# Startup loads, order of the modulation groups, start points of small jobs and of the context stream in a fused two-block transformer kernel

## The reference, cut to what matters

```python
for l in range(2):                                    # first block
    x = layer_norm(a * x + 0.5 * swiglu_ffn(x, w_in[l, 0], w_out[l, 0]), ...)
    x = layer_norm(a * x + mixer_sublayer(x, ...), ...)
    x = layer_norm(a * x + memory_cross_attention(x, mem, ...), ...)
    x = layer_norm(a * x + 0.5 * swiglu_ffn(x, w_in[l, 1], w_out[l, 1]), ...)
for l in range(2):                                    # second block; the context's last use is as keys of layer 1
    sh_a, sc_a, g_a, sh_f, sc_f, g_f = split(silu(cond) @ mod_w[l] + mod_b[l], 6)
    hx, hc = modulate(rms_norm(x), sh_a, sc_a), modulate(rms_norm(ctx), ...)
    y_x, y_c = even_mixer(hx, hc) if l == 0 else odd_mixer(hx, hc)
    x = x + g_a * (y_x @ w_out[l]);  x = x + g_f * swiglu(modulate(rms_norm(x), sh_f, sc_f), ...)
    # the context likewise, in layer 0 only
```

## Time and profile before

| | |
|---|---|
| median of 3 runs | 2775.28 us (2775.11 to 2776.57) |
| the profiled execution, its own time | 2772.24 us |
| its span, first to last instruction | 2770.4 us |
| mean granted TensorE clock | 0.986 |
| busy: PE, DVE, ACT, POOL | 2653.8, 1682.5, 1239.3, 171.5 us |

### The profile page before, as it was taken

How to read it: one execution, slowest core, us unless ns; L and a number is a source line. 1 busy time by engine, 2 the same in 40 slices (tenths; PEclk the granted TensorE clock), 3 DMA queues, 4 the chain that set the end, 5 groups by cost and what they waited for, 6 DMA issues and landing times. The chain is left out here.

```text
span 2770.4 us, 47510 instructions
## 1 busy us (share of the span) xinstructions
PE 2653.8 (96%) x16073; PEld 2215.4 (80%) x16073; DVE 1682.5 (61%) x2451; ACT 1239.3 (45%) x1731; POOL 171.5 (6%) x205
## 2 busy tenths in 40 slices
PE   8999999999989999999989998999999997899999
PEld 8987878879969978778688886877896884665898
DVE  5555675755545565767565767875664654755655
ACT  4444544444324445354344654555443442543443
POOL 0000000000120000000000201200000001100000
PEclk9999999999989999999999999999999998999999
DMA  7656455566766574456556535543555557433664
GB/s 235 187 186 188 130 163 182 191 213 190 203 212 199 163 233 127 142 171 202 200 182 184 154 122 169 164 141 106 162 187 185 198 163 209 138 99 122 206 190 137
DMA packets 250509, 480.32 MB, mean 173 GB/s; under 512 B 16697, under 2 KB 36225, under 8 KB 250273
## 3 DMA queue, kind: packets, MB, share of 16 engines
q1 hardware_dynamic: 239968, 444.19, 51.2%
q0 software_dynamic: 10304, 33.09, 4.2%
HBM read 470.37 MB, written 7.74 MB: 173 GB/s over the span
## 5 line engine op out<-in xcount | busy, mean ns | idle before, releaser
L121 DVE TENSOR_TENSOR wlo<-raw,whi 128x1024 fp32r<-128x1024 f32 (+2 forms) x786 | 914.2, 1173 | 766.5 <-ACT whi L162 618.7
L162 ACT ACTIVATE whi<-raw 128x1024 fp32r<-128x1024 f32 (+2 forms) x786 | 791.0, 1016 | 695.1 <-PE bank L170 533.5
L170 PE MATMUL bank<-xh,whi 128*128 128x256 f32 x2208 | 631.4, 286 | 16.5 <-DVE xl L121 9.4
L170 PE MATMUL bank<-xh,wlo 128*128 128x256 f32 x2208 | 627.2, 284 | 0.0
L170 PE MATMUL bank<-xl,whi 128*128 128x256 f32 x2208 | 626.3, 284 | 0.0
L170 PEld LDWEIGHTS bank<-xh,whi 128*128 128x128 f32 x2208 | 420.4, 190 | 33.9 <-issue 16.2
L170 PEld LDWEIGHTS bank<-xl,whi 128*128 128x128 f32 x2208 | 418.8, 190 | 1.1 <-issue 0.5
L170 PEld LDWEIGHTS bank<-xh,wlo 128*128 128x128 f32 x2208 | 419.2, 190 | 0.0
L170 PE MATMUL bank<-whi,xh 128*128 128x512 f32 (+2 forms) x632 | 257.5, 407 | 25.6 <-DVE wlo L121 6.7
L170 PE MATMUL bank<-wlo,xh 128*128 128x512 f32 (+2 forms) x632 | 248.8, 394 | 0.0
L170 PE MATMUL bank<-whi,xl 128*128 128x512 f32 (+2 forms) x632 | 248.7, 394 | 0.0
(11 more groups left out here) (415 smaller groups left out, 3841.9 us busy)
## 6 DMA issues: line engine op xcount, KB each, us to landing
raw<-in_ffn_w_in SPq DMA_DIRECT2D x280, 512.0 KB, 4.4
raw<-in_ffn_w_out SPq DMA_DIRECT2D x154, 512.0 KB, 4.3
raw<-in_w_mix_in SPq DMA_DIRECT2D x112, 512.0 KB, 3.6
raw<-in_mod_w SPq DMA_DIRECT2D x96, 512.0 KB, 4.7
raw<-in_od_w_in SPq DMA_DIRECT2D x40, 512.0 KB, 4.4
raw<-in_ffn_w_in SPq DMA_DIRECT2D x56, 256.0 KB, 2.8
raw<-in_w_branch SPq DMA_DIRECT2D x24, 512.0 KB, 3.6
raw<-in_ev_w_in SPq DMA_DIRECT2D x24, 512.0 KB, 3.7
```

The source lines that it names most:

```text
L121: return Made(self.e and self.e.tensor_tensor(out, a, b, op))
L162: return Made(self.e and self.e.activation(out, a, f, **k))
L170: return Made(self.e and self.e.matmul(out, lhs, rhs, **k))
```

## The change

x is loaded by SP in four pieces of 256 columns, ahead of and between the first weight blocks, and each piece is transposed on its own; the identity is loaded apart from the other constants, and the first layer norm's rows wait for these. The modulation groups go in another order, in which a gate's group never follows a gate's group, and the numbers that streams wait for follow. `rpb_scratch`, `tokens_of`, `dsa` and `choose_last` get one or more `yield`s. The context stream starts 12 us later by the planner. The context's values of the odd layer (two products, eight blocks) wait until x's feed-forward of the even layer is done. The odd layer's gate rows are loaded by a job.

```diff
+GROUPS = (0, 1, 2, 3, 4, 6, 5, 7, 8, 10, 9, 11)
+def for_norm(l, f):
+    return 12 * l + (11 if f else 4)
+def for_gate(l, f):
+    return 12 * l + (12 if f else 7)
@@ modulation
-        for j in range(12):
-            blk, half, i = j // 2, j % 2, j % 2
+        for place_, j in enumerate(GROUPS):
+            blk, half, i = j // 2, j % 2, place_ % 2
...
@@ setup
-    co.cdep = load_small(co, co.cst[:, :], A["consts"][:, :])
-    co.xready = load_small(co, co.x[:, :, :], A["x"][0].rearrange("(t p) d -> p t d", p=P))
-    load_ln(co, 0, 0)
-    co.xt.dep = to_t(co, lambda t, k: co.x[:, t, k * P:(k + 1) * P], 8, (co.xt.hi, co.xt.lo),
-                   (co.xready, co.cdep))
+    idep = load_small(co, co.cst[:, C_ID:C_ID + P], A["consts"][:, C_ID:C_ID + P])
+    co.cdep = load_small(co, co.cst[:, P:C_END], A["consts"][:, P:C_END])
...
+    for i in range(4):
+        cs = slice(256 * i, 256 * i + 256)
+        co.xready.append(co.sp.dma_start(co.x[:, :, cs], x[:, :, cs]).then_inc(co.s_x[i], by=16))
+        if i < AHEAD:
+            stage(co, i)
+        co.xt.dep += to_t(co, lambda t, k: co.x[:, t, (2 * i + k) * P:(2 * i + k + 1) * P], 2, ...)
+    load_ln(co, 0, 0, co.cdep)
@@ rpb_scratch
     a = co.dv.memset(z[:, :], 0.0).then_inc(co.s_dv)
+    yield
...
     for r in range(7):
+        yield
+        yield
         src = A["na_rpb_2"][0, :, r + 4, :]
@@ prenorm
-    yield from modulated(co, 12 * l + 6 * f + 4)
+    yield from modulated(co, for_norm(l, f))
@@ context
     ev.start(fe)
+    yield -12
...
     for c in range(2):
         yield from co.od.heads_gemm(1, 1, c, c1)
+    yield from until(co, "x fed")
+    for c in range(2):
         yield from co.od.values_gemm(1, c, c1)
@@ rows
     yield from ffn2(co, 0, 0, x2, gate, tiles)
+    co.passed.add("x fed")
...
+    gate = Gate(co.lg, co.pn.tile[:, 0:512], counts(co))
+    def gate_early():
+        while co.modulated < for_gate(1, 0):
+            yield
+        gate.make = gated(co, 1, 0, 0, gate)
+    early = spawn(co, gate_early())
     first = spawn(co, od.attend(0, co.Y, pr, at_, co.smo, co.mxo, counts(co), ya))
...
     last = spawn(co, od.attend(1, co.Y, pr, at_, co.smo, co.mxo, counts(co), yb))
-    yield from modulated(co, 18)
-    gate = Gate(co.lg, co.pn.tile[:, 0:512], counts(co))
-    make = gated(co, 1, 0, 0, gate)
-    yield from out_proj(co, 1, 0, 4, co.xt, make)
+    yield from modulated(co, for_gate(1, 0))
+    while not early.over:
+        yield 0
+    yield from out_proj(co, 1, 0, 4, co.xt, gate.make)
```

More of the change, by code:

```diff
@@ L224, in new_core @@
     co.s_out = sem("s_out")
+    co.s_x = [sem(f"s_x{i}") for i in range(4)]
     co.s_raw = [sem(f"s_raw{i}") for i in range(NRAW)]
@@ L241, in new_core @@
     co.bi = 0
-    for u in range(AHEAD):
-        stage(co, u)
     return co
@@ L803, in modulation @@
                 if late is not None and n == 1:
-                    m, half0, a, r = late
-                    rfree[r] = mod_columns(co, m // 12, m % 12 // 2, half0, rt[r], a)
-                    co.modulated, late = m + 1, None
+                    at, blk0, half0, a, r = late
+                    rfree[r] = mod_columns(co, at // 12, blk0, half0, rt[r], a)
+                    co.modulated, late = at + 1, None
                 yield took
@@ L814, in modulation @@
                     gate_bias(co, gates)
-                co.modulated = 12 * l + j + 1
+                co.modulated = 12 * l + place_ + 1
             else:
-                late = (12 * l + j, half, got[0], i)
+                late = (12 * l + place_, blk, half, got[0], i)
 def mod_columns(co, l, blk, half, rows, ready):
@@ L954, in setup @@
     co.xfree = co.rsfree = None
-    co.cdep = load_small(co, co.cst[:, :], A["consts"][:, :])
-    co.xready = load_small(co, co.x[:, :, :], A["x"][0].rearrange("(t p) d -> p t d", p=P))
-    load_ln(co, 0, 0)
-    co.xt.dep = to_t(co, lambda t, k: co.x[:, t, k * P:(k + 1) * P], 8, (co.xt.hi, co.xt.lo),
-                   (co.xready, co.cdep))
+    idep = load_small(co, co.cst[:, C_ID:C_ID + P], A["consts"][:, C_ID:C_ID + P])
+    co.cdep = load_small(co, co.cst[:, P:C_END], A["consts"][:, P:C_END])
+    x = A["x"][0].rearrange("(t p) d -> p t d", p=P)
+    co.xready, co.xt.dep = [], []
+    for i in range(4):
[3 more added lines that the diff above has]
+            stage(co, i)
+        co.xt.dep += to_t(co, lambda t, k: co.x[:, t, (2 * i + k) * P:(2 * i + k + 1) * P], 2,
+                          (co.xt.hi[:, 2 * i:2 * i + 2, :], co.xt.lo[:, 2 * i:2 * i + 2, :]), (co.xready[i], idep))
+    load_ln(co, 0, 0, co.cdep)
 def side_setup(co, fe):
@@ L973, in gen @@
         outs, made = [], []
-        co.dv.wait_ge(d, fe)
+        co.dv.wait_ge(d, fe, co.cdep)
         for h in range(8):
@@ L1793, in gated @@
 def gated(co, l, s, f, gate):
-    assert co.modulated >= 12 * l + 6 * f + 6
+    assert co.modulated >= for_gate(l, f)
     st = co.stream[s]
@@ L2384, in context @@
     yield from turned(co, room, 0, 8, tuple(done), c2, da_gain(co))
-    yield from modulated(co, 6)
+    yield from modulated(co, for_gate(0, 0))
     gate = Gate(at(74, "cgb", [P, D]), at(78, "cgw", [P, 512]), w["first block"])
@@ L2506, in rows @@
     yield from turned(co, co.Y, 4, 8, tuple(yb), co.xt)
-    yield from out_proj(co, 1, 4, 8, co.xt, make)
+    yield from out_proj(co, 1, 4, 8, co.xt, gate.make)
     co.limit, co.pn.free = 24, gate.free
```

## The result

| | median us | runs |
|---|---|---|
| before, beside it on the same chip | 2775.20 (2771.04 to 2776.78) | 6 |
| after | 2759.05 (2757.30 to 2761.66) | 6 |

The ratio is 0.9944, 95% interval 0.9931 to 0.9957: faster by 16 us, where 37 were forecast, and outside the range of 2720 to 2757. The profiled execution took 2757.32 us by its own time, with a span of 2755.5.

What follows compares the result with a forecast made beforehand. PE's own work was taken to bound the kernel, leaving its idle and half-clock time to win. Gains summed to 41.1 us, less 4.0 for new stalls: 2775.3 - 37.1 = 2738.2 us, range 2720 to 2757.

Steps and rivals of the forecast that it cites:

- Start: Kernel start: x loaded in pieces lets the first product start between 10.6 and 13.1 us; gain 0.5 us, from -0.5 to 4.0.
- One more block before a small job goes on: Mixer, both layers: an added product block covers PE's waits at `tk`, `ikt` and `choose_last`; gains 3.6, 1.8 and 8 us.
- DVE bounds the mixer: Rival: the mixer's stalls only move by a block; 13.4 us fewer gained, 2752 us; chance 0.12.
- about 1.6 us for each layer: Mixer, `choose_last`: stall left at the second score products, from stalls of 3.32 and 3.79 us, with PE arriving at about 363.2.
- The other terms, 3.6 and 1.8: Mixer, both layers: 3.6 us from the `tk` transposes' wait for DVE's copy, 1.8 us from the wait for `ikt`.
- Scratch transfers: Stall of 4.41 us at 765.99 behind seven scratch transfers: yields leave POOL's issues together; gain 0.
- Gate groups apart: PE's 6.30 us stall at 808.19 and 3.1 us of clock go; gain 8.5 us, from 6 to 9.4.
- The context later: Context's first transposes: starting 12 us later covers the 5.03 us stall at 1397.90; gain 5.0 us, from 4 to 7.
- The values held back: x's odd pre-norm: eight values blocks replace modulation, 10.0 us lost instead of 21.2; gain 11.2 us.
- Gate rows: Odd layer, `out_proj`: modulation forced ahead removes the 1.89 us stall, the 4.02 may stay; gain 2.5 us, from -3 to 8.
- New small stalls: Where two streams are woven, shifts make two new stalls of 1.89 us; 4.0 us taken off the gain.
- The slower rival: Context's attention: 19 shifted steps wait for their exponentials, deciding from 2.0 us each; 2786 us at 2.5; chance 0.05.

Runs made afterwards that it cites:

- experiment 1: Kernel after without the yields in `tokens_of`, `dsa` and `choose_last`: 2754.44 us, ratio to before 0.9926.
- experiment 10: Kernel after without the mixer's three yields and with DVE's wait for `tbias` two blocks later: 2751.70 us, ratio to before 0.9914.
- Experiments 2 to 5: Feed-forward counts taken ahead of small loads on the kernel after: 2750.34 us; on the kernel before, new group order 2769.45, early counts 2774.57, the two together 2764.43 us.
- order 5.3: Kernel before with only the new order of modulation groups and the numbers waited for: 2769.45 us, ratio to before 0.9984.
- counts 1.8: Kernel before with only the feed-forwards' "everything so far" counts taken ahead of the small loads: 2774.57 us, ratio to before 0.9993.
- both 11.9: Kernel before with the new group order and the counts taken ahead of the small loads: 2764.43 us, ratio to before 0.9951.
- experiment 6: Kernel before with only the gap of 12 us of planned work ahead of the context's first pre-norm: 2774.52 us, ratio to before 0.9997.
- experiment 9: Kernel after with the odd layer's twelve `nb` mask loads put behind x's pre-norm: 2760.45 us, ratio to before 0.9942.
- Experiment 8: Kernel before with only the context's values of the odd layer held back until x's feed-forward is done: 2757.12 us, ratio to before 0.9938.
- experiments 11 and 12: Kernel after with early counts, the mixer's three yields removed and DVE's bias wait two blocks later: 2746.71 us; the same without the context's 12 us gap: 2746.72 us.

## Why the prediction was wrong

Of the 37.1 us, 14.9 came in the profiled executions. By the prediction's own steps:

- **Start** (0.5): right, 0.9. The first feed-forward ends at 210.1 to 211.2 us in the kernels with the new start and at 211.2 to 212.1 in those with the old one. The first product starts at 12.39, between the bounds of 10.6 and 13.1, and runs at the slow pace at first (0.21 us from one product to the next).
- **One more block before a small job goes on** (3.6 + 1.8 + 8 = 13.4): wrong, -3.8, and 17 us of the 22 that are missing. This is the rival "DVE bounds the mixer", which had 0.12, and worse than it, since it was priced at nothing gained. The failed step is the stall of "about 1.6 us for each layer", worked out from PE arriving "at about 363.2". The ready block is ahead of the stall, but PE arrived at 361.1 and stalled 3.45 us, because the transfer came no earlier than before: DVE's wait for `tbias` ended at 360.57 after and at 360.74 before. What PE had gained up to there it stood again. The 3.3 us of clock for each layer did not come either. The other terms, 3.6 and 1.8, came as stalls gone and were taken back by the new ones on `zs`, `qlt` and `sg` (experiment 1 undoes both). The prediction named DVE's wait as the cause and then priced an edit that leaves it in place; taking that wait later removes the stall (experiment 10), and its idle time is given back on `sg`.
- **Scratch transfers** (0): right. POOL's row is unchanged with the yields alone, and so is the time. The 1.5 us of this stretch are noise: kernels without these yields came out between 2.0 us shorter and 0.2 longer than before in it, and the stall behind the transfers lay between 3.5 and 5.8 us without the yields and between 4.2 and 6.7 with them.
- **Gate groups apart** (8.5): the stall at 808 did go, and the size was right for its removal (9.3 us once nothing was behind it). The failed step is "6.30 + 3.1 us of clock are gone" without a look at what is late next. ACT's 7.16 us wait for the small loads stood in the trace of before, ended 20 us after the stall, and cost only 0.25 us there because PE was late already. Experiments 2 to 5 show it: order 5.3, counts 1.8, both 11.9.
- **The context later** (5.0): too large, 0.9 in the change. In the seven traced kernels with the gap this stretch is 0.8 to 2.3 us shorter than before, and 0.0 to 1.2 longer in the six others without it, so the gap gains some 2 us there. In the time 1.1 and 0.0 us of it show (experiments 6 and 12), neither clear of noise. In experiment 6 the stall itself fell by 4.4 us; small stalls on DVE's steps of the attention took its place. "What is late next" was answered with the margin at the end of the stretch (21.2 us), which held, and not with the steps in between. Why each of these steps is later was not taken apart.
- **The values held back** (11.2): right in size, 12.7. Inside it, seven blocks of modulation left the place and not eight, the stall on y was 2.5 us and not 6.9, since two blocks more ran before it, and four stalls of 4.7 us together came later that were not foreseen. The cause named for y, POOL's queue of mask loads, is shown (experiment 9).
- **Gate rows** (2.5): 1.9. Experiment 8 has a gain of 3.5 in that stretch without the gate job, so nothing shows that the job gains anything; it was not tried by itself. The prediction called the move of the values and of modulation neutral, which experiment 8 does not bear out by these 3.5 us.
- **New small stalls** (4.0): two of 1.89 us were assumed; those counted above show that this was too little, but they are already in the stretches' numbers.

The slower rival, attention steps that wait for their exponentials at 2.0 us each, did not come: of the steps only a few wait, for 0.3 to 1.4 us on `pc`.

## What to carry to other kernels

Before a stall is booked as gain, look for waits on the other engines that end within the next 20 us, even those that cost nothing now: here a wait of ACT that cost PE 0.25 us became a 5 us stall as soon as PE came earlier, and the two edits together were worth 11.9 us where they gave 5.3 and 1.8 alone. Time gained ahead of a wait is kept only where what it waits for comes earlier too: more work ahead of the consumer left the late transfer as it was, while an edit at the wait itself removed the stall. Undo the edits one by one when a change bundles several: here one of them gave all of the gain. A "wait for everything so far" is to be taken ahead of unrelated loads.

## What the runs showed of the hardware

- The mask loads keep the DMA engines busy at a low rate: a share of 1.04 at 202 to 216 GB/s while they run, against 1.01 at 387 GB/s in the earlier trace rows. They take 12.4 us (median) from issue to landing in the kernel after, with weights at 5.5 us beside them.
- In the kernel after, the clock over the 7 us behind a stall of 3.45 us was 0.51 (at 364 us) and behind one of 3.32 us 0.76 (at 392 us): the length of the stall alone did not tell it. Behind 1.44 us at 1406 it stayed at 1.00.
- The kernels of experiments 11 and 12 have the same program up to the context. Behind a stall of 2.03 us in the one and of 2.00 us in the other, before the same products, the clock over the next 7 us was 1.00 and 0.76:

```profile
386.20:393.20 7.00, 7.00 (x32) 5.52 (x33) 4.48 (x6) 4.72 (x6) 0.54 (x1) 1.00 0.68 193
386.94:393.94 7.00, 7.00 (x26) 5.74 (x27) 4.39 (x6) 4.82 (x6) 0.54 (x1) 0.76 0.66 192
```
